# Differential attention on one Trainium2 core: the third query tile is scaled ahead of the fourth tile's maxima

## The reference, cut to what matters

```python
s1 = einsum('bqhd,bkhd->bhqk', qb1, k1) * scale + bias   # bias = -slope * |i - j|
s2 = einsum('bqhd,bkhd->bhqk', qb2, k2) * scale + bias
p = softmax(s1) - lam * softmax(s2)
out = einsum('bhqk,bkhe->bqhe', p, v)
```

## Time and profile before

| what | value |
|---|---|
| median of 3 runs | 1434.49 us |
| profiled execution, its own time | 1434.86 us |
| its span, first to last instruction | 1433.0 us |
| TensorE matmul busy | 1414.8 us (99%) |
| VectorE busy | 1020.2 us (71%) |
| ScalarE busy | 707.4 us (49%) |
| mean granted TensorE clock | 0.998 |
| chain that ended last, share of the span | PE 89%, DVE 4%, ACT 2%, DMA 2% |

### The profile page before, as it was taken

One profiled execution on the slowest core, in us unless ns is written; L12 is line 12 of the kernel. 1 busy time (PEld: TensorE's weight loads), 2 busy tenths in 40 slices (PEclk: granted clock), 3 DMA queues, 4 the chain that ended last, 5 costly groups with the idle time before them and its releaser, 6 DMA issues.

```text
span 1433.0 us, 17881 instructions
## 1 busy us (share of the span) xinstructions
PE 1414.8 (99%) x6604; PEld 1175.1 (82%) x6604; DVE 1020.2 (71%) x1381; ACT 707.4 (49%) x894; POOL 31.5 (2%) x52
## 2 busy tenths in 40 slices
PE   8999999999999999999999999999999999999997
PEld 7888888888888888888888877888888888888886
DVE  6967888898878768666766755665667353478966
ACT  6546334544443466665666666555564222324434
POOL 0000000000000000000000000000000000000000
PEclk9999999999999999999999999999999999999999
DMA  8439586767765642223232434322242444617674
GB/s 299 145 125 317 174 262 186 250 197 224 224 198 193 199 133 81 74 82 86 80 90 81 102 112 124 81 74 66 81 140 73 148 123 156 206 45 247 192 248 179
DMA packets 182976, 218.43 MB, mean 152 GB/s; under 512 B 19456, under 2 KB 133248, under 8 KB 182272
## 3 DMA queue, kind: packets, MB, share of 16 engines
q1 hardware_dynamic: 174304, 197.64, 44.7%
q10 hardware_dynamic: 8608, 19.93, 3.6%
HBM read 195.51 MB, written 22.02 MB: 152 GB/s over the span
## 4 chain that ended last, share of the span: by engine, by line
PE 89%; DVE 4%; ACT 2%; DMA 2%; issue 1%; SPq 1%; POOL 0%; ACTq 0%; DVEq 0%; POOLq 0%
PE duo L2100 27%; PE duo L2102 27%; PE duo L2101 27%; PE duo L2153 2%; DMA start_y<-start_columns 1%; PE duo L2127 1%; PE duo L2130 1%; SPq L610 1%; ACT m_hi L886 1%; PE duo L2144 1%; PE duo L2149 1%; PE duo L2146 1%; PE duo L2148 1%; PE duo L2145 1%; PE duo L2583 0%
## 5 line engine op out<-in xcount | busy, mean ns | idle before, releaser
L1375 DVE TENSOR_TENSOR w_lo<-w_raw,w_hi 128x1024 fp32r<-128x1024 f32 (+1 forms) x116 | 135.3, 1167 | 103.4 <-ACT w_hi L781 102.7
L2100 PE MATMUL duo<-h_hi,w_hi 128*128 128x512 f32 x512 | 201.8, 394 | 0.0
L2102 PE MATMUL duo<-h_hi,w_lo 128*128 128x512 f32 x512 | 199.8, 390 | 0.0
L2101 PE MATMUL duo<-h_lo,w_hi 128*128 128x512 f32 x512 | 199.7, 390 | 0.0
L886 ACT ACTIVATE m_hi<-m_raw 128x2048 fp32r<-128x2048 f32 (+1 forms) x66 | 115.5, 1752 | 144.3 <-PE duo L2102 71.5
L781 ACT ACTIVATE w_hi<-w_raw 128x1024 fp32r<-128x1024 f32 (+1 forms) x118 | 119.1, 1011 | 126.6 <-DMA w_raw<-in_w_ob_dram 65.8
L1492 DVE TENSOR_TENSOR m_lo<-m_raw,m_hi 128x2048 fp32r<-128x2048 f32 (+3 forms) x71 | 141.9, 2001 | 26.3 <-ACT m_hi L886 25.8
L2100 PE MATMUL duo<-m_hi,h_hi 128*128 128x512 f32 x368 | 144.6, 393 | 1.6 <-DVE h_lo L1528 1.1
L2102 PE MATMUL duo<-m_hi,h_lo 128*128 128x512 f32 x368 | 143.3, 389 | 0.0
L2100 PE MATMUL duo<-m_hi,s_hi 128*128 128x512 f32 x320 | 124.5, 389 | 0.0
L2102 PE MATMUL duo<-m_hi,s_lo 128*128 128x512 f32 x320 | 124.5, 389 | 0.0
(11 more groups left out here) (322 smaller groups left out, 2977.8 us busy)
## 6 DMA issues: line engine op xcount, KB each, us to landing
m_raw<-in_w_in_dram SPq DMA_DIRECT2D x110, 512.0 KB, 4.7
w_raw<-in_w_in_dram SPq DMA_DIRECT2D x132, 256.0 KB, 3.2
o_raw<-in_w_out_dram SPq DMA_DIRECT2D x32, 512.0 KB, 5.0
spare<-in_w_in_dram SPq DMA_DIRECT2D x17, 512.0 KB, 4.8
h_raw<-in_w_in_dram SPq DMA_DIRECT2D x17, 512.0 KB, 5.0
w_raw<-in_w_oa_dram SPq DMA_DIRECT2D x32, 256.0 KB, 3.4
sig<-gates SPq DMA_DIRECT2D x8, 1024.0 KB, 6.4
w_raw<-in_w_ob_dram SPq DMA_DIRECT2D x32, 256.0 KB, 3.3
```

Source lines behind the costliest of these rows:

```text
L1375: dve.tensor_tensor(w_lo[:, piece.slot, 0:cols], w_raw[:, piece.slot, 0:cols], w_hi[:, piece.slot, 0:cols].bitcast(F32), ALU.subtract).the ...
L2100: pe.matmul(dst, lhs_hi, rhs_hi, start=start, stop=False)
L2101: pe.matmul(dst, lhs_hi, rhs_lo, start=False, stop=False)
L2102: return pe.matmul(dst, lhs_lo, rhs_hi, start=False, stop=stop)
```

## The change

In step 1 VectorE does the scaling of the third tile before it takes the maxima of the fourth tile. No instruction is added, removed or changed; the waits inside the two helpers stay as they are. The line is common to all heads, the one behind the last head too.

```diff
                     pt_lo(h - 1, 0, TR)
                     max_a(h - 1, 2, first)
                     pt_lo(h - 1, 1, TR)
+                    norm_a(h - 1, 2)
                     max_a(h - 1, 3, first)
-                    norm_a(h - 1, 2)
```

## The result

The changed kernel takes 1438.05 us (median of 8 runs, 1435.69 to 1438.53); the kernel before took 1433.28 beside it (8 runs, 1432.01 to 1434.76). The ratio is 1.0029, with a 95% interval of 1.002 to 1.0038: slower by 4.2 us (2.9 to 5.4); the bare medians lie 4.8 apart. The profiled execution took 1438.0 us, its span is 1436.2 (before 1433.0).

A forecast was written before the change was run, and what follows sets the result against it. TensorE was taken to bound the kernel, busy 1414.8 of 1433.0 us. Middle heads 2.0, first head 1.4 and last head 1.2 sum to 4.6 us on 1434.86, less 0.37 for the median: 1439.1, range 1436.7 to 1441.2.

The forecast's parts named there:

- the last head's term: Last head: SyncE's loads issued 1.6 us later make ScalarE's weight piece late; TensorE +1.2 us, bounds -0.3 and 1.6.
- The wait that goes: Third transpose, each head: TensorE's wait for the third tile's scaling disappears, 0.19 us in each of six middle heads.
- A chain with no play in it: Behind the fourth tile's maxima, ScalarE and VectorE work up to the third tile's low half all moves 1.65 us later.
- not slower: Rival: VectorE's 0.90 us idle time takes the shift, so the gains of 2.5 us stand: 1432.0; chance 0.05.
- The cost at the fourth transpose: Middle heads: its load waits for the third tile's low half, 0.53 us; net +0.34 per head, 2.0 for six.
- The rule d - 0.16: At the transposes: a weight load starting d us after the last projection matmul costs TensorE d - 0.16 us.
- The first head: VectorE is full there: 0.34 at the transposes, 0.6 at the product, 0.45 at the feature sums; +1.4 us in all.
- only the middle heads pay: Rival: rotary work and the load have unseen play; 7 x 0.34 = 2.4, less up to 0.3: 1436.8; chance 0.14.
- The 1 MB beside them moves along, so the 7.5 should hold: Last head: weight-piece loads issued 1.6 us later, the second still landing 7.5 us after issue.
- VectorE alone would give about 0: Last head, case of loads landing earlier for the same issue: VectorE, full there, gives about 0 at 849.53.
- second fall: Rival: clock halves again, by the last head's 1.6 us wait or the first head's three: +1.7, 1440.8; chance 0.10.
- The present fall: Half clock for 3.4 us behind the 2.3 us wait at 868; rival that it goes: +2.9, 1437.4; chance 0.07.

The follow-up runs named there:

- experiment 4: Changed kernel, with the fourth tile's scaling also moved up, right behind the fourth tile's maxima, in all heads: 1432.82 us, ratio 0.9997 to the kernel before.
- experiment 7: As experiment 4, but with the old order in the first head: 1432.77 us, ratio 0.9992 to the kernel before.
- experiment 5: Kernel before (old order) with one more VectorE instruction, 0.68 us, in step 2: 1434.64 us, ratio 1.0007 to the kernel before.
- experiment 6: Changed kernel (new order) with one more VectorE instruction, 0.68 us, in step 2: 1442.11 us, ratio 1.0059 to the kernel before.
- Experiment 2: Kernel before with the new order only in the first head: 1435.18 us, ratio 1.0007 to the kernel before.
- experiment 3: Kernel before with the new order only in the last head: 1433.20 us, ratio 1.0000 to the kernel before.
- Experiment 9: Changed kernel with SyncE's weight piece put ahead of the wait for the last maxima and the compressed-row load behind it: 1437.35 us, ratio 1.0025 to the kernel before.
- experiment 8: As experiment 7, with two of ScalarE's copies of values made earlier, behind the heads: 1431.71 us, ratio 0.9986 to the kernel before.
- experiment 10: Kernel before with only two of ScalarE's copies of values made earlier, behind the heads: 1433.34 us, ratio 0.9995 to the kernel before.
- experiment 12: As experiment 8, with the load order of Experiment 9: 1430.97 us, ratio 0.998 to the kernel before.

## Why the prediction was right, and where it was not

The forecast was 1439.1 in 1436.7 to 1441.2, slower; 1438.05 was measured. The mechanism in the first seven heads is shown by the runs; the last head's term was wrong. That the total comes so close (4.6 us forecast, 4.2 measured) is in part luck: the marks give 3.58, 1.0 less than forecast, and something outside the sum (the last point below) made up for a part of it.

- **The wait that goes.** Right: 0.18 in a middle head. With no wait at the fourth transpose to take it back it is worth 0.2 per head (experiments 4 and 7).
- **"A chain with no play in it."** Right: 7.15 us for 7.14 from the negation to the low half, a shift of 1.65, and VectorE's idle time grew from 0.90 to 2.54 and absorbed nothing. Experiments 5 and 6 show that the old order had play and the new one has none. The rival "not slower" rested on that idle time and falls.
- **The cost at the fourth transpose.** 0.59, and 0.53 was predicted: the load starts 0.11 behind the low half, and I had taken 0.05 from the load that waits for the scaling. The rule d - 0.16 held (d = 635.03 - 634.28 = 0.75). A middle head costs 0.38 for 0.34, six of them 2.28 for 2.0. I had looked for the new wait as PEld's for line 1386; the profile books it to line 1421.
- **The first head.** 1.44, as predicted. By the distances the product's wait costs 0.66 and the sums' 0.45, against 0.6 and 0.45 forecast, though the profile books only 0.39 and 0.20 of idle time to them. With 0.38 for the transposes, as in a middle head, that is 1.49 for the 1.44 measured. Experiment 2 gives +1.42 by itself. The rival "only the middle heads pay" falls by it.
- **The last head is the step that failed.** Predicted +1.2, measured -0.14 (+0.16 in experiment 3), within the bounds of -0.3 to 1.6. "The 1 MB beside them moves along, so the 7.5 should hold": it did not; the second load landed 5.6 us behind its issue, and ScalarE took the piece 0.06 late and not 1.6. ScalarE was also ready for it earlier than before, as TensorE had turned the compressed rows 1.06 earlier, and that is why it still shows a wait of 1.20. With that, VectorE was the one that ended last; "VectorE alone would give about 0" was the case that came. Experiment 9 shows it by removing the load's wait and changing nothing. In experiment 6 the load took 7.6 us and the head cost 1.35, so the price given was that of the slow load, and the error was to take one reading of a load for its value.
- **The clock.** No second fall came behind waits of up to 1.6 us. The present fall is in the changed kernel's profile too. The difference of the times by their ratio (4.2 us) is 0.6 above that of the marks. A different share of executions with the fall can be the rest. Of the changed kernel's eight, two took 1435.69 and 1436.36 with a mean granted clock of 0.999, six 1437.44 to 1438.53 with 0.997 or 0.998. Of the eight of the kernel before, five lie at 1432.01 to 1433.32 and three at 1434.03 to 1434.76. If the upper groups are those with the fall, which costs 1.7 (an estimate: 3.4 us at half the clock), three executions more in eight are worth 0.6. No run here settles it, as the clocks of those eight are not on record.

## What to carry to other kernels

Before you move an instruction earlier in a full in-order queue, follow what it passes to the next point at which the bounding engine needs something of it, and add up the play there: here 1.15 us stood against a shift of 1.65. Idle time on the queue absorbs a shift only if it is waiting for something that the shift does not move; work that can be put into this idle time (the fourth tile's scaling) is what turns such a loss into a gain. A DMA's latency from one trace is one sample; if a term of the sum hangs on it, ask what ends next if it is 2 us shorter.

## What the hardware showed that I had not expected

**One wait, two outcomes.** Of the 14 profiles (before, after, twelve experiments) eleven have the 2.35 us wait ahead of the place of the earlier trace rows undivided. In seven of these the clock then fell to half (1.2 of 2.4 GHz) for 3.4 us; in four (experiments 3, 4, 6 and 7) it stayed full behind the same wait. The windows of the changed kernel and of experiment 7 behind that wait (us of the window, busy us of PE, PEld, DVE, ACT, POOL with their counts, granted clock, DMA share, GB/s):

```profile
868.00:872.00 4.00, 1.65 (x8) 1.06 (x7) 2.02 (x4) 3.57 (x5) 0.00 (x0) 1.00 0.00 0
872.00:876.00 4.00, 4.00 (x12) 3.19 (x11) 3.75 (x6) 1.63 (x4) 0.00 (x0) 0.58 0.35 131
```

```profile
864.00:868.00 4.00, 1.82 (x8) 1.51 (x9) 3.20 (x5) 2.72 (x5) 0.00 (x0) 1.00 0.17 66
868.00:872.00 4.00, 4.00 (x20) 3.30 (x19) 2.57 (x4) 1.71 (x4) 0.00 (x0) 1.00 0.41 134
```

Twelve matmuls in four us at a mean clock of 0.58, twenty at the full one. In none of the three with the wait divided (experiments 8, 10, 12) did it fall. Nor did it fall behind the wait of 2.61 us in the last head of experiment 6, which is longer than the one that it fell behind. The stretch behind the marks takes 582.3 to 582.9 us in the seven profiles with the fall and 580.6 to 581.9 in the seven without it. What decides between the two outcomes is open. So is whether each fall lengthens an execution: experiment 6's four took 1442.05 to 1442.20 us, three of them with a mean clock of 0.997 and the slowest with 0.999.

**A load's time varies by more than the shift.** The same second weight load behind the compressed rows took 7.5 us from issue to landing in the kernel before, 5.6 in the changed one and 7.6 in experiment 6. In the twelve profiles with this order of loads, ten lie between 5.4 and 6.1, and only the kernel before and experiment 6 are above. The prediction was worked out from one of the two long ones. With the compressed rows behind it (experiments 9 and 12) it took 3.7 and 3.8.
